# Sixteen dense tokens of the expert value stage are gathered, in packed form, instead of multiplied

## The chip, the cores and the metric

The kernel runs on one core of a Trainium2 chip and computes the whole step in one launch. The metric is the device time of that launch in microseconds (us). Before the change it was 4382.22 us, the median of three runs (4379.09 to 4385.64).

## The reference, cut to what matters

One layer of a hybrid decoder trunk is run for 576 tokens of width 2048 (512 of the prompt, 64 of eight samples). After the mixers (gated linear attention, mLSTM, S5) comes PEER, a layer of 16384 experts that are one neuron each. Every token has 8 heads, every head picks 16 experts, so a token has 128 picks:

```python
u_sel = jnp.take(u_tab, eidx, axis=0)
act = jax.nn.gelu(jnp.einsum('bhkd,bd->bhk', u_sel, xb))
v_sel = jnp.take(v_tab, eidx, axis=0)
return jnp.einsum('bhk,bhkd->bd', gate * act, v_sel)
```

`gate` is a softmax over the 16 scores of a head. Then `x = x + gate2 * out`, and a final RMSNorm over the 2048 channels.

## The kernel before, in words

All of the kernel's large products are made in three parts: each fp32 factor is split into a rounded high part and a low rest, and TensorE multiplies high by high, high by low and low by high, in the fp32r type. ScalarE writes the high parts, VectorE the low ones.

The kernel treats the 576 tokens in two ways. Tokens 0 to 319 (`TD` = 320) are **dense**; tokens 320 to 575 (256 of them, `TR`) are **rows**.

- First pass over the u table, `rows_product` (L2348 to L2362): for the 256 row tokens the activations of all 16384 experts are computed and saved to `row_activation_scratch`. Beside it VectorE picks the experts of all five token tiles in the order `ROUTED` = (3, 4, 0, 1, 2). Tiles 3 and 4 are the row tokens; their picks are written as indices (`row_ids`, `act_ids`). Tiles 0 to 2 cover the dense tokens.
- Second pass over the u table, `block_product`: 128 blocks of 128 experts, 48 matmuls each with 320 columns of dense tokens; ScalarE saves gelu of each block to `activation_scratch`. During its first 60 blocks (`GBLK * GL`) a matrix of gates, expert by token, is built for the dense tokens from one-hot matrices: VectorE makes them (`one_hots`, L1839 to L1845), TensorE multiplies them (L2429), ScalarE copies them out. PE may start block n only when VectorE has made its low part (`low`, L1719).
- Value stage (L2437 to L2462): the value table is read in 256 units (`UNITS`) of 128 experts by 1024 channels. A unit is 8 x 3 matmuls (L2457, L2458, L2459) with 320 columns, whose moving operands are the coefficients (gate times activation) of the dense tokens. Eight units make a round; after each, VectorE adds eight PSUM banks to `acc` (`add_half`, L1890). Per unit, SP loads the values (ring of six), ScalarE makes `ev_hi` (ring of four, L1204), VectorE makes `ev_lo` (L1869). Every second round also makes eight sets of coefficients (L1875, L1211, L1879).

The row tokens are **gathered**: for pick number s of 128, one token per partition, GpSimd (POOL) fetches one activation per partition (`act_column`, L793) and one value row of 2048 channels per partition (`value_rows`, L800). VectorE multiplies and adds them into `acc_rows` (`add_rows`, L1835, the first of a tile at L1832). That is 256 gathers (`NSP`) for two tiles of 128 tokens. POOL issues in the order of its program: 16 activation columns, then for each s the activation column s + 16 and the value rows s. All instructions of VectorE are in the order of the program too, and `add_rows` calls stand at fixed places in it: the first 56 (`NSP_GATES`) one behind each of the last 56 `low` calls of the 60 gate blocks, so behind that of b = 4 at first; up to number 148 (`NSP_EARLY`) in the remaining blocks of the second pass, the other 108 in the value stage, at most one per unit and only in units 2 to 6 of a round.

At the end TensorE transposes the gathered sums (`turn_rows`, twelve channel groups first, the last four between the sums of squares), VectorE scales both kinds of sum with `gate2` and adds them to x (L1919, L1931, L1935, L1936), TensorE sums the squares (L2480), VectorE scales the output (L1941).

Of the kernel before, what the change touches and what calls it, by code (L numbers as in the profile page):

```python
# [7 lines left out]
ALU = mybir.AluOpType  # L8
ACT = mybir.ActivationFunctionType
AX = mybir.AxisListType  # L10
F32 = mybir.dt.float32
# [22 lines left out]
TR = T - TD  # L34
RND = 8
UNITS = 2 * NK
RAWS, HIS, COS, ROWS = 6, 4, 11, 4
NSP, NSP_GATES, NSP_EARLY = 256, 56, 148
# [38 lines left out]
def build(nc, a, o):  # L77

    ctx = ExitStack()
    with ctx:  # L80
# [177 lines left out]
        gates = [attw[:, 128 * k:128 * k + 128] for k in range(2)]  # L258
        row_ids = [attw[:, 256 + 128 * k:384 + 128 * k].bitcast(U32) for k in range(2)]
        acts = [attw[:, 512:640], gla_mask[:, :].bitcast(F32)]  # L260
        act_ids = [cap[:, :].bitcast(U32), siluc[:, 0:128].bitcast(U32)]
        tcol = siluc[:, 128:130]
# [29 lines left out]
        acc_rows = [h_rest[:, :, TD + P * k:TD + P * k + P] for k in range(2)]  # L292
# [5 lines left out]
        smp = at(24064 + 2 * T, 4 * TS).rearrange("p (c b t) -> p c b t", c=4, t=SLEN)  # L298
        assert C0 + 12 * T <= C0 + ROWS * D and 8 * TD >= 4 * T
# [33 lines left out]
        act_table = rd.rearrange("k p (t o) -> (k p t) o", o=1)  # L333
        v_table = a["peer_v"].rearrange("i p d -> (i p) d")
# [61 lines left out]
        cols_made, idx_made, act_in = sem("cols_made"), sem("idx_made"), [sem(f"act{k}_in") for k in range(2)]  # L396
# [35 lines left out]
        VB = (6, 7, 4, 5, 0, 1, 2, 3)  # L432

# [73 lines left out]
        def _(sp):  # L507
# [118 lines left out]
            def load_factors(q):  # L626
                if q >= 2:
                    sp.wait_ge(co_lo_made, 4 * (q - 1))
                sp.dma_start(ag_acts[q % 2].rearrange("p (i t) -> p i t", t=TD), ad[:, 4 * q:4 * q + 4]
                             ).then_inc(ag_in[q % 2], 16)  # L630
                sp.dma_start(ag_gates[q % 2], gd[:, :, 4 * q:4 * q + 4, :]).then_inc(ag_in[q % 2], 16)
# [29 lines left out]
        def _(pool):  # L661
# [126 lines left out]
            pool.sem_inc(cols_made, 1)  # L788


            def act_column(c):
                k, s = c // P, c % P
                pool.indirect_dma_start(out=acts[k][:, s:s + 1], out_offset=None, in_=act_table,  # L793
# [3 lines left out]
            def value_rows(s):  # L797
                if row_clear(s):
                    pool.wait_ge(rows_used, row_clear(s))
                pool.indirect_dma_start(out=v_rows[row_place(s)], out_offset=None, in_=v_table,  # L800
                                        in_offset=bass.IndirectOffsetOnAxis(ap=row_ids[s // P][:, s % P:s % P + 1], axis=0)
# [17 lines left out]
        def _(act):  # L819
# [386 lines left out]
            def coefficient_high(n):  # L1206
# [4 lines left out]
                act.activation(co_hi[n % COS][:, :], ag_acts[n // 4 % 2][:, TD * (n % 4):TD * (n % 4) + TD], ACT.Copy  # L1211
                               ).then_inc(co_hi_made, 1)

            value_high(0)
# [23 lines left out]
        def _(dve):  # L1238
# [520 lines left out]
            for turn, n in enumerate(ROUTED):  # L1759
# [39 lines left out]
                if n < 3:  # L1799
                    ins.then_inc(sel_made, 1)  # L1800
                    next_low()
                    dve.wait_ge(sel_made, n + 1)
                    continue
                step(ins)
                next_low()
                dve.wait_ge(cols_made, 1)
# [13 lines left out]
            def add_rows(s):  # L1820

                if s == 0:
                    dve.wait_ge(blk_made, NB_ROWS)
                if s % ACOL == 0:
                    g, part = s // ACOL, slice(s % P, s % P + ACOL)
                    dve.wait_ge(act_in[g % 2], 16 * ACOL * (g // 2 + 1))
                    step(tt(acts[s // P][:, part], acts[s // P][:, part], gates[s // P][:, part], ALU.mult))
                k, col = s // P, acts[s // P][:, s % P:s % P + 1]
                row = v_rows[row_place(s)].rearrange("p (c t) -> p c t", t=P)
                dve.wait_ge(rows_in[row_sem(s)], row_fills(s))  # L1830
                if s in (0, P):
# [40 lines left out]
            def coefficients(q):  # L1872
                dve.wait_ge(ag_in[q % 2], 32 * (q // 2 + 1))
                x4 = ag_acts[q % 2].rearrange("p (i n t) -> p n i t", i=4, t=TBLK)
                tt(x4, x4, ag_gates[q % 2], ALU.mult).then_inc(co_made, 1)  # L1875

            def coefficient_low(n):
                dve.wait_ge(co_hi_made, n + 1)
                tt(co_lo[n % COS][:, :], ag_acts[n // 4 % 2][:, TD * (n % 4):TD * (n % 4) + TD],  # L1879
                   co_hi[n % COS][:, :].bitcast(F32), ALU.subtract).then_inc(co_lo_made, 1)  # L1880
# [677 lines left out]
```

## Time and profile before

| what | value |
|---|---|
| median of three runs | 4382.22 us |
| the profiled execution's own time | 4366.72 us |
| its span | 4365.0 us |
| PE busy | 4230.0 us (97%) |
| VectorE busy | 2829.1 us (65%) |
| ScalarE busy | 1289.3 us (30%) |
| POOL busy | 982.6 us (23%) |
| mean DMA rate | 228 GB/s |

The profile is of one execution. Its engines are PE (matmul), PEld (weight load, overlapping PE), DVE (VectorE), ACT (ScalarE), POOL (GpSimd), SP (the DMA queue of loads). "L12" is line 12 of the kernel. A matmul's duration overlaps the next one's, so the pace of matmuls is read from start to start. "DMA share" is the mean busy share of 16 DMA engines.

### The profile page before, as it was taken

Reading aid. Unit: us, or ns where it says so; the run is one execution under the profiler, and the core shown is the slowest. Engines: PE = TensorE matmul, PEld = TensorE weight load, DVE = VectorE, ACT = ScalarE, POOL = GpSimd, SP = SyncE. Lnnn points to the kernel's source line nnn. Section 1 sums busy time; section 2 is a strip of 40 time slices with the busy share of each in tenths; the row PEclk is TensorE's granted clock in tenths of the full one; section 3 lists DMA queues with packets and bytes.
Section 4 is the critical chain, followed back from the end, with each engine's and each line's share of the span. In section 5 each row is a group of like instructions: output and inputs, shape, how many; then the busy total and the mean of one; then the engine's idle time right before and its main releaser. Section 6 shows DMA issues by size and latency. Waiting matters only on the chain.

```text
span 4365.0 us, 63107 instructions
## 1 busy us (share of the span) xinstructions
PE 4230.0 (97%) x26448; PEld 3767.1 (86%) x26448; DVE 2829.1 (65%) x3861; ACT 1289.3 (30%) x1402; POOL 982.6 (23%) x627
## 2 busy tenths in 40 slices
PE   6999999999999899999999999999999999999997
PEld 3777777776689798777777999999999999999996
DVE  2488311322443424888888688877777688888885
ACT  2000101211221312443344444443333333333332
POOL 1000000001100100000000322228777355545430
PEclk8999999998889899999999999999999999999999
DMA  9211112127942223666666788889999999999984
GB/s 390 49 58 59 64 65 68 39 77 273 342 177 101 77 76 118 209 209 203 207 207 207 245 313 317 313 313 400 383 386 383 333 330 329 334 335 326 334 313 149
DMA packets 295940, 994.31 MB, mean 228 GB/s; under 512 B 42696, under 2 KB 112008, under 8 KB 233528
## 3 DMA queue, kind: packets, MB, share of 16 engines
q1 hardware_dynamic: 208728, 652.83, 42.9%
q0 software_dynamic: 48320, 279.88, 16.6%
q10 hardware_dynamic: 38688, 58.73, 3.6%
q8 instruction: 146, 2.39, 0.2%
q14 instruction: 58, 0.48, 0.0%
HBM read 917.71 MB, written 73.64 MB: 227 GB/s over the span
## 4 chain that ended last, share of the span: by engine, by line
PE 85%; DMA 7%; DVE 6%; ACT 2%; issue 0%; POOL 0%; SPq 0%; DVEq 0%; ACTq 0%
PE PS L2209 13%; PE PS L2334 8%; PE PS L2335 8%; PE PS L2336 8%; PE PS L2457 7%; PE PS L2459 7%; PE PS L2458 7%; PE PS L2212 5%; DMA arena<-in_peer_ut 5%; PE PS L2359 3%; DVE blk_lo L1719 3%; PE PS L2361 3%; PE PS L2360 3%; PE PS L1972 2%; PE PS L2429 2%; PE PS L2315 2%
## 5 line engine op out<-in xcount | busy, mean ns | idle before, releaser
L1719 DVE TENSOR_TENSOR blk_lo<-arena,blk_hi 128x2048 fp32r<-128x2048 f32 x272 | 623.3, 2292 | 252.6 <-ACT blk_hi L1093 249.8
L2334 PE MATMUL PS<-h_hi,blk_hi 128*128 128x320 f32 (+1 forms) x2496 | 773.7, 310 | 2.1 <-DVE blk_lo L1719 1.2
L2335 PE MATMUL PS<-h_lo,blk_hi 128*128 128x320 f32 (+1 forms) x2496 | 765.9, 307 | 0.0
L2336 PE MATMUL PS<-h_hi,blk_lo 128*128 128x320 f32 (+1 forms) x2496 | 765.8, 307 | 0.0
L800 POOL DMA_INDIRECT arena<-in_peer_v,attw x256 | 486.6, 1901 | 806.7 <-DVE arena L1835 729.5
L1093 ACT ACTIVATE blk_hi<-arena 128x2048 fp32r<-128x2048 f32 x272 | 520.7, 1914 | 401.1 <-DMA arena<-in_peer_ut 400.1
L2457 PE MATMUL PS<-co_hi,ev_hi 128*128 128x320 f32 x2048 | 634.3, 310 | 4.7 <-DVE ev_lo L1869 2.5
L2458 PE MATMUL PS<-co_lo,ev_hi 128*128 128x320 f32 x2048 | 633.8, 309 | 0.0
L2459 PE MATMUL PS<-co_hi,ev_lo 128*128 128x320 f32 x2048 | 633.7, 309 | 0.0
L2209 PE MATMUL PS<-arena 128*128 128x288 f32 x2176 | 552.4, 415 | 2.1 <-DVE arena L1278 2.1
L2209 PEld LDWEIGHTS PS<-arena 128*128 128x128 f32 x2176 | 417.6, 194 | 121.0 <-issue 2.6
L2334 PEld LDWEIGHTS PS<-h_hi,blk_hi 128*128 128x128 f32 x2496 | 470.1, 188 | 3.9 <-issue 1.9
L2335 PEld LDWEIGHTS PS<-h_lo,blk_hi 128*128 128x128 f32 x2496 | 470.0, 188 | 0.0
L2336 PEld LDWEIGHTS PS<-h_hi,blk_lo 128*128 128x128 f32 x2496 | 469.5, 188 | 0.0
L1204 ACT ACTIVATE ev_hi<-arena 128x1024 fp32r<-128x1024 f32 x256 | 271.8, 1062 | 568.5 <-DMA arena<-in_peer_v 318.9
L2359 PE MATMUL PS<-blk_hi,h_hi 128*128 128x512 f32 x1024 | 408.4, 399 | 21.2 <-DVE blk_lo L1719 21.1
L793 POOL DMA_INDIRECT attw<-row_activation_scratch,cap x128 | 183.3, 1432 | 999.3 <-DMA row_activation_scratch<-arena 960.5
L2360 PE MATMUL PS<-blk_hi,h_lo 128*128 128x512 f32 x1024 | 400.1, 391 | 0.0
L2361 PE MATMUL PS<-blk_lo,h_hi 128*128 128x512 f32 x1024 | 400.0, 391 | 0.0
L2457 PEld LDWEIGHTS PS<-co_hi,ev_hi 128*128 128x128 f32 x2048 | 385.0, 188 | 5.5 <-DVE ev_lo L1869 3.1
L2458 PEld LDWEIGHTS PS<-co_lo,ev_hi 128*128 128x128 f32 x2048 | 385.0, 188 | 0.0
L2459 PEld LDWEIGHTS PS<-co_hi,ev_lo 128*128 128x128 f32 x2048 | 384.9, 188 | 0.0
(455 smaller groups left out, 5992.7 us busy)
## 6 DMA issues: line engine op xcount, KB each, us to landing
arena<-in_peer_ut SPq DMA_DIRECT2D x256, 1024.0 KB, 6.0
arena<-in_peer_v SPq DMA_DIRECT2D x256, 512.0 KB, 6.9
arena<-in_w_ada SPq DMA_DIRECT2D x38, 2048.0 KB, 11.3
arena<-in_w_f SPq DMA_DIRECT2D x17, 2048.0 KB, 7.9
activation_scratch<-arena ACTq DMA_DIRECT2D x128, 160.0 KB
gate_scratch<-arena ACTq DMA_DIRECT2D x10, 2048.0 KB, 14.4
arena<-activation_scratch SPq DMA_DIRECT2D x32, 640.0 KB, 7.7
arena<-gate_scratch SPq DMA_DIRECT2D x32, 640.0 KB, 11.0
```

Of the source, the lines that this page charges most:

```text
L1093: act.activation(blk_hi[k][:, :], blk_raw[k], ACT.Copy).then_inc(blk_hi_made, 1)
L1719: tt(blk_lo[k][:, :], blk_raw[k], blk_hi[k][:, :].bitcast(F32), ALU.subtract).then_inc(blk_lo_made, 1)
L2209: ins = mm(bank(job % 2, 0, HALF), w[:, c, P * (j // 2):P * (j // 2) + P], hT[:, c, HALF * (j % 2):HALF * (j % 2) + HALF], start=c == 0, s ...
L2334: mm(out, hi[:, c], h_part[0][:, c, cols], start=c == 0, stop=False)
L2335: mm(out, hi[:, c], h_part[1][:, c, cols], start=False, stop=False)
L2336: ins = mm(out, lo[:, c], h_part[0][:, c, cols], start=False, stop=c == KC - 1)
L2359: mm(out, h_part[0][:, 4 * q + c, tok], hi[:, c], start=first, stop=False)
L2360: mm(out, h_part[1][:, 4 * q + c, tok], hi[:, c], start=False, stop=False)
L2361: ins = mm(out, h_part[0][:, 4 * q + c, tok], lo[:, c], start=False, stop=last)
L2457: mm(out, ev_hi[k % HIS][:, w], co_hi[n % COS][:, :], start=i == 0, stop=False)
L2458: mm(out, ev_hi[k % HIS][:, w], co_lo[n % COS][:, :], start=False, stop=False)
L2459: ins = mm(out, ev_lo[k % RAWS][:, w], co_hi[n % COS][:, :], start=False, stop=i == RND - 1)
```

## The change

Tokens 304 to 319 (`NX` = 16) leave the dense value product, which now has 304 columns (`TV`), and are gathered as well. Sixteen tokens with 128 picks each are 2048 rows, packed as 16 gathers of 128 partitions: partition 16 g + t holds a pick of token t, and eight groups of partitions take eight picks of each token at a time. So there are 272 gathers. Numbers 208 to 223 are the new ones.

- After tile 2 is routed, VectorE computes row index, activation index and gate for it (five small instructions), and POOL packs them with eight small DMAs. These stand in POOL's program after its first 16 activation columns and before the first value rows.
- The activations of the sixteen tokens are fetched from `activation_scratch`, which still holds all 320 columns; the u pass is not changed, nor are the loads of coefficients (ten groups of 32 tokens).
- `NSP_GATES` goes from 56 to 58 and `NSP_EARLY` from 148 to 152, so the first `add_rows` stands behind the `low` of b = 2, and 120 of them are in the value stage.
- At the end a matmul with a fixed 128 x 16 matrix (`part_sum`) adds the eight groups of partitions for each of 16 channel groups, and VectorE adds the result to x. The turned rows use eight slots of PSUM in place of twelve, so groups 8 to 11 wait for the first quarter of VectorE's final sums, and groups 12 to 15 for the second.

```diff
-NSP, NSP_GATES, NSP_EARLY = 256, 56, 148
+NSP, NSP_GATES, NSP_EARLY = 256 + NX, 58, 152
+X_FIRST = 208
...
-            pool.wait_ge(sel_made, 3)
+            pool.wait_ge(idx_made, 3)
+            lo = TV - TILE_AT[2]
+            for g in range(XPARTS):
+                pool.dma_start(packed[NX * g:NX * g + NX].rearrange("p (r k) -> p r k", k=NX),
+                               unpacked[lo:lo + NX, :, NX * g:NX * g + NX]).then_inc(pack_in, 16)
             for s in range(NSP):
+                if s + ACOL == X_FIRST:
+                    pool.wait_ge(pack_in, 16 * XPARTS)
+                    for k in range(3):
+                        pool.wait_ge(a_saved[k], saves(NB_ALL)[k])
                 if s + ACOL < NSP:
                     act_column(s + ACOL)
...
-                    out, w = bank(VB[c], 0, TD), slice(P * c, P * c + P)
-                    mm(out, ev_hi[k % HIS][:, w], co_hi[n % COS][:, :], start=i == 0, stop=False)
+                    out, w = bank(VB[c], 0, TV), slice(P * c, P * c + P)
+                    mm(out, ev_hi[k % HIS][:, w], co_hi[n % COS][:, 0:TV], start=i == 0, stop=False)
...
             def turn_rows(c):
-                slot = c % 12
-                if c >= 12:
-                    pe.wait_ge(fin_made, 1)
+                slot = c % 8
+                if c in (8, 12):
+                    pe.wait_ge(fin_made, c // 4 - 1)
+                mm(bank(4 + c // 4 % 2, NX * (c % 4), NX), acc_rows[2][:, c], part_sum, start=True, stop=True)
...
+                step(tt(few, bank(4 + q % 2, 0, 4 * NX).rearrange("p (c t) -> p c t", t=NX),
+                        mod[:, 80 + 4 * q:84 + 4 * q, 0:1].broadcast_to([P, 4, NX]), ALU.mult))
+                tt(xg[q][:, :, TV:TD], xg[q][:, :, TV:TD], few, ALU.add)
```

## Rows read from the trace of the kernel before

**Rows 1.** Page, part 4: the chain that ended last, by engine.
```profile
PE 85%; DMA 7%; DVE 6%; ACT 2%; issue 0%; POOL 0%; SPq 0%; DVEq 0%; ACTq 0%
```

**Rows 2.** Windows: gate blocks, rest of second pass, value stage; columns in the first line.
```profile
core 0: us, PE busy (x) PEld busy (x) DVE busy (x) ACT busy (x) POOL busy (x), PEclk, DMA share, GB/s
3412.30:4317.90 905.60, 903.00 (x6144) 902.41 (x6144) 746.81 (x785) 317.54 (x382) 410.09 (x191) 1.00 0.88 319
2435.10:2934.00 498.90, 498.90 (x3559) 498.90 (x3558) 422.25 (x359) 227.84 (x203) 150.29 (x129) 1.00 0.84 306
2934.00:3411.00 477.00, 474.89 (x3228) 473.03 (x3226) 363.43 (x166) 154.69 (x134) 354.94 (x192) 1.00 0.99 385
```

**Rows 3.** Timeline of PE, query blocks: start us, us, instruction; 256, then 320 columns.
```profile
1554.64 0.28 PE L2335 MATMUL PS<-h_lo,blk_hi 128*128 128x256 f32 x1
...
1560.28 0.31 PE L2334 MATMUL PS<-h_hi,blk_hi 128*128 128x320 f32 x1
...
1567.32 1.27 PE L2370 MATMUL PS<-arena 128*128 x10
```

**Rows 4.** Timeline of POOL: first gathers, and two plain DMAs earlier.
```profile
924.85 0.53 POOL L752 DMA_DIRECT2D out_m_s<-arena  x1
...
2457.06 1.90 POOL L793 DMA_INDIRECT attw<-row_activation_scratch,cap  x1 [0.30 <-issue]
...
2460.51 0.97 POOL L793 DMA_INDIRECT attw<-row_activation_scratch,cap  x1 [0.30 <-issue]
...
2469.40 0.94 POOL L800 DMA_INDIRECT arena<-in_peer_v,attw  x1 [0.30 <-issue]
```

**Rows 5.** Timeline of DVE, start of the gate blocks.
```profile
2455.86 2.29 DVE L1719 TENSOR_TENSOR blk_lo<-arena,blk_hi 128x2048 fp32r<-128x2048 f32 x1
...
2470.24 2.29 DVE L1719 TENSOR_TENSOR blk_lo<-arena,blk_hi 128x2048 fp32r<-128x2048 f32 x1 [1.97 <-ACT blk_hi L1093]
...
2476.35 1.29 DVE L1832 TENSOR_SCALAR arena<-arena,attw 128x2048 f32<-128x2048 f32 x1 [3.73 <-DMA arena<-in_peer_v,attw]
2477.55 0.69 DVE L1843 TENSOR_TENSOR arena<-iota,arena 128x512 f32<-128x512 f32 x1
```

**Rows 6.** Timeline of ACT there: the gelu behind the end of block b = 3.
```profile
2467.97 0.44 ACT L1104 ACTIVATE arena<-PS 128x320 f32<-128x320 f32 x1 [0.70 <-PE PS L2336]
```

**Rows 7.** PE after a long idle time: timeline, and the window behind it.
```profile
1467.24 0.55 PE L2394 MATMUL PS<-h_hi,blk_hi 128*128 128x256 f32 x1 [15.54 <-DVE h_lo L1713]
...
1467.20:1472.30 5.10, 5.06 (x21) 5.09 (x22) 4.75 (x5) 5.10 (x7) 0.00 (x0) 0.50 0.00 0
```

**Rows 8.** Timeline of ACT and PE at unit 21 of the value stage.
```profile
3488.23 1.06 ACT L1204 ACTIVATE ev_hi<-arena 128x1024 fp32r<-128x1024 f32 x1 [9.45 <-DMA arena<-in_peer_v]
...
3490.60 0.42 PE L2457 MATMUL PS<-co_hi,ev_hi 128*128 128x320 f32 x1
```

**Rows 9.** Windows: one round without and one with coefficients to make.
```profile
3469.00:3497.00 28.00, 27.98 (x191) 27.72 (x190) 20.36 (x19) 8.49 (x8) 11.91 (x10) 1.00 0.99 368
3497.00:3525.00 28.00, 28.00 (x193) 28.00 (x192) 26.55 (x31) 11.20 (x16) 15.68 (x7) 1.00 0.88 306
```

**Rows 10.** DMA view of 3440 to 4290 us: packets, MB, share; issues and us to landing.
```profile
q0 software_dynamic: 17587, 108.06, 32.5%
...
arena<-in_peer_v,attw POOLq DMA_INDIRECT x103, 10.0
```

**Rows 11.** Groups by line of 3440 to 4290 us: busy, mean ns, idle before.
```profile
L1835 DVE SCALAR_TENSOR_TENSOR arena<-arena,gla_mask 128x2048 f32<-128x2048 f32 x107 | 251.1, 2347 | 0.2
```

**Rows 12.** Timeline, the end (DVE, PE) and a matmul with 8 columns.
```profile
1035.62 1.95 PE L2282 MATMUL PS<-arena 128*128 128x8 f32 x16
...
4313.79 3.79 DVE L1919 SCALAR_TENSOR_TENSOR arena<-arena,modT 128x320 f32<-128x320 f32 x8 [7.39 <-DMA arena<-x_scratch]
...
4322.07 0.42 DVE L1931 TENSOR_TENSOR arena<-PS,modT 128x256 f32<-128x256 f32 x1 [1.32 <-PE PS L2471]
...
4325.03 1.29 PE L2480 MATMUL PS<-arena,ones 128*128 128x512 f32 x4 [1.31 <-ACT arena L1233]
```

More of the change, by code:

```diff
@@ L34 @@
 TR = T - TD
+NX = 16
+TV = TD - NX
+XPARTS = P // NX
+VGROUPS = -(-TV // TBLK)
 RND = 8
@@ L257, in build @@
         e_f, a_f = p_rep[:, 0:P], p_rep[:, P:2 * P]
[L258 to L262, printed above, removed]
+        packed = scaleg[:, 0:3 * NX]
+        gates = [attw[:, 128 * k:128 * k + 128] for k in range(2)] + [packed[:, 2 * NX:3 * NX]]
+        row_ids = [attw[:, 256 + 128 * k:384 + 128 * k].bitcast(U32) for k in range(2)] + [packed[:, 0:NX].bitcast(U32)]
+        acts = [attw[:, 512:640], gla_mask[:, :].bitcast(F32), scaleg[:, 3 * NX:4 * NX]]
+        act_ids = [cap[:, :].bitcast(U32), siluc[:, 0:128].bitcast(U32), packed[:, NX:2 * NX].bitcast(U32)]
+        tcol = siluc[:, 128:131]
+        unpacked = at(R1, 3 * P).rearrange("p (r k) -> p r k", k=P)
+        part_sum = silu32[:, 0:NX]
         p_sv = sel_all[:, 0:256].rearrange("p (h s k) -> p h s k", s=2, k=TOPK)
@@ L291, in build @@
         h_rest = at(KC * T, KC * T).rearrange("p (c t) -> p c t", t=T)
-        acc_rows = [h_rest[:, :, TD + P * k:TD + P * k + P] for k in range(2)]
+        acc_rows = [h_rest[:, :, TD + P * k:TD + P * k + P] for k in range(2)] + [h_rest[:, :, 0:P]]
         v_rows = [at(C0 + D * k, D) for k in range(ROWS + 1)]
@@ L395, in build @@
         ev_made, vp_made, acc_made = sem("ev_made"), sem("vp_made"), sem("acc_made")
-        cols_made, idx_made, act_in = sem("cols_made"), sem("idx_made"), [sem(f"act{k}_in") for k in range(2)]
+        pack_in, idx_made, act_in = sem("pack_in"), sem("idx_made"), [sem(f"act{k}_in") for k in range(2)]
         rows_in = [sem(f"rows{k}_in") for k in range(ROWS)]
@@ L787, in _ @@
                                allow_small_or_imprecise_dtypes=True))
-            pool.sem_inc(cols_made, 1)
+            step(pool.iota(tcol[:, 2:3], [[0, 1]], base=TILE_AT[2], channel_multiplier=1,
+                           allow_small_or_imprecise_dtypes=True))
+            step(pool.tensor_copy(part_sum, ident[:, 0:NX]))
+            for g in range(1, XPARTS):
+                step(pool.tensor_tensor(part_sum, part_sum, ident[:, NX * g:NX * g + NX], ALU.add))
+            pool.sem_inc(consts_made, 1)
             def act_column(c):
-                k, s = c // P, c % P
-                pool.indirect_dma_start(out=acts[k][:, s:s + 1], out_offset=None, in_=act_table,
+                k, s = row_of(c)
+                pool.indirect_dma_start(out=acts[k][:, s:s + 1], out_offset=None, in_=act_table if k < 2 else dense_table,
                                         in_offset=bass.IndirectOffsetOnAxis(ap=act_ids[k][:, s:s + 1], axis=0)
@@ L797, in value_rows @@
             def value_rows(s):
+                k, col = row_of(s)
                 if row_clear(s):
```

55 lines of the change are left out of this document (36 added, 19 removed).

## The prediction

> **What bounds the kernel now.** I read the chain of waits first: 85% of it is PE [rows 1]. Then the windows by stage. In the gate blocks PE is busy all 498.9 us, in the rest of the second pass 474.9 of 477.0, in the value stage 903.0 of 905.6 [rows 2]. So what matters there is how long a matmul takes, and whether something makes PE wait. The other columns show what stands close behind: in the rest of the second pass the DMA engines are busy 0.99 of the time at 385 GB/s, in the value stage 0.88, and VectorE there 746.8 of 905.6 us.
>
> **Fewer columns.** Matmuls overlap, so their pace is the distance of starts. In the query blocks the same instructions run with both widths: 47 steps of 256 columns take 1560.28 - 1554.64 = 5.64 us, 120.0 ns each; 48 steps of 320 columns take 1567.32 - 1560.28 = 7.04 us, 146.7 ns each [rows 3]. That is 0.417 ns per column, so 304 columns take 146.7 - 16 x 0.417 = 140.0 ns. The value stage has 6144 of them (905.6 / 6144 = 147.4, the same pace [rows 2]). Gain: 6144 x 6.67 ns = **-41.0 us**. A unit falls from 3.52 to 3.36 us, a round from 28.2 to 26.9. The widths on both sides were measured; only if the pace had a step between 256 and 320 columns could the gain be 0 or 164 us, and neither end is near.
>
> **The first gather meets an earlier place in VectorE's order.** This is the term that I take to be most important after the columns. Before, the first `add_rows` stands behind the low part of b = 4, which starts at 2470.24, and VectorE still waits 3.73 us for the first rows (2476.35) [rows 5]. Now it stands behind that of b = 2, which starts at 2455.86 and ends at 2458.1. But POOL does not start earlier: its first column waits for the saved activations of the first pass. Column 10 starts at 2457.06, column 12 at 2460.51, and each costs 0.94 and 0.30 between them where nothing disturbs it; at that pace from column 11 (2459.3) on, column 16 ends at 2466.4. Then come the eight packing DMAs, 0.53 us each by a plain small one: 4.3 us; one more column 1.25; the first value rows 1.25, issued at 2473.2 [rows 4]. Before, the rows were issued at 2470.34 and VectorE went on 6.0 us later [rows 4, 5]. So they land at about 2479.2, with little other traffic perhaps 1.5 us earlier.
>
> VectorE executes in order, and behind the waiting `add_rows` stand the one-hots (three instructions of 0.7) and the low part for block b = 4 of the gate blocks. PE has finished block 3 at about 2467.6, by the gelu of 2467.97 [rows 6], and needs that low part then. It gets it at 2479.2 + 1.2 (first multiply) + 2.1 (one-hots) + 2.3 (low) = 2484.8: PE idles 17.2 us; with the faster landing 15.7. I take 16.5, bounds 12 and 21 (packing DMAs of 0.3 to 1.0 us). After 15.5 us without work PE ran at a granted clock of 0.50 (1.2 GHz) for 5.1 us [rows 7]; half of that is lost, 2.5 us. Nothing gives this back, as PE is busy all the time afterwards [rows 2]. **+19 us.** The next blocks: VectorE owes per block one low part 2.2, one `add_rows` 2.3 and 4/3 one-hots 2.8 us, 7.3 in all, against some 8 us of PE, so no second stall. The five instructions at the end of routing (some 1.5 us) lie where VectorE waits for ScalarE; nothing.
>
> **Two more gathers in the rest of the second pass** (94 for 92). A gather with its column costs 32.5% of 850 us over 103, 2.7 us of all DMA engines [rows 10]; two are 5.4 us in 477 that are 0.99 full [rows 2]. The bounds are 0 (the rows only queue longer; POOL is four ahead) and 6. I take **+2**, since PE there loses 2 us of 477 at this load.
>
> **Twelve more gathers in the value stage** (120 for 108). On VectorE each is 2.26 us (2347 ns, of which 0.09 overlap [rows 11]): +27, and the narrower sums and coefficients give back 6. So 768 of 864.6 us, 89% for 82%. A round with coefficients had 26.55 us of work in 28 [rows 9]; with 0.37 more gathers and 16 narrower instructions (0.3) it has 27.1 against 26.9. The round without them has 20.4 and takes the rest. VectorE is up to three units ahead, so alone it costs about nothing (0 to 3).
>
> The DMA engines are the closer matter. Their share was 0.88 x 905.6 = 797 us, plus 12 x 2.7 = 829 of 864.6: 0.96. But rounds differ: where coefficients are loaded the engines are busy 0.99 of a round at 368 GB/s, in the other 0.88 [rows 9]. In the full ones loads arrive late already: at unit 21 the cast starts at 3488.23 after waiting 9.45 us for its load, and the unit's first matmul, at 3490.60, lasts 0.42 where the others of its kind last 0.31 [rows 3, 8]: it had to wait a little, there is no reserve at all. A round shorter by 1.3 us with 1.0 us (0.37 x 2.7) more to move makes loads 2.3 us later. Reading the casts against PE's units in all sixteen such rounds, four had under 2 us of reserve and ten over 3; so four lose about 2 us each and a few some tenths. I take **+7**, bounds 0 and 16.
>
> One rule of the Trainium skill speaks against the change: its page "DMA: Bandwidth & Descriptors", section "Specifications", gives about 358 GB/s as the limit that HBM sets per core. By it the full rounds (368 x 28 us = 10.3 MB, plus 0.4) would need 29.9 us instead of 26.9, and the stage would lose some 48 us rather than 7. The trace does not agree: it moved 385 GB/s over 477 us [rows 2].
>
> **The end.** The loads of x are issued six units before the end and land when VectorE then still has 3.8 us of work before its last half round [rows 12]; six units are now 1.0 us shorter, the sums 0.3 shorter: +0.7. Each channel group now has one more fp32 matmul with 16 columns. Sixteen instructions of eight such matmuls with 8 columns took 1.95 us, so 0.23 each [rows 12]. Four of them delay VectorE's first quarter (4322.07) by 0.9, two more small instructions cost 0.5, and that quarter takes 2.2; the four groups that now wait for its end (4325.7) take 0.45 each, and the sums of squares begin at 4327.6, not at 4325.03 [rows 12]: +2.6, and 4 x 0.23 between them. In all **+4.2** with x, bounds 2 and 7.
>
> **Sum.** -41.0 + 19 + 2 + 7 + 4.2 = -8.8 us against the profiled time of 4366.7. That execution was 15.5 us under the median of the runs; the difference carries over unchanged, so 4382.2 - 8.8 = **4373.4**, say 4373. From the bounds (the terms' ends rarely come together) the case's own range is 4358 to 4388.
>
> **Rivals.**
> 1. *The transfers bound the value stage* (slower). Full rounds can't lend to the others, because the ring of loads is only six units deep. Each of sixteen stays at its 28 us times 0.99 plus 1.0 = 28.7 in place of 26.9: 29 us lost, where I put 7. 4373 + 22 = 4395. For: rows 8 and 9. Against: 385 GB/s was possible [rows 2], so the 10.7 MB need only 27.8. The change is slower by more than 0.2% once the stage's losses pass 25 us.
> 2. *The first gather is hidden*: POOL or the activations come earlier, or PE has more low parts in stock than I read. Then 19 goes: 4354. For: the wait of 3.73 us before hurt nobody. Against: PE needs the low part right behind the waiting instruction.
> 3. *The value stage keeps its pace*, with the stall at the first gather as forecast: 4366. For: the second pass runs at 0.99 with PE hardly waiting [rows 2].
> 4. *Columns don't set the pace in this stage*, so 304 cost what 320 do (the change doesn't do what it says): 4414. Against: rows 3.
> 5. *Full rounds stay at the rate they had*, rival 1 in a sharper form: 10.7 MB at the 368 GB/s of [rows 9] are 29.1 us, 2.2 lost in each of sixteen, 35 in place of 7: 4401. The page "DMA: Bandwidth & Descriptors" of the Trainium skill (Specifications) would set that rate at 358.
>
> **How the numbers follow.** Forecast 0.55, rival 1 0.10, rival 5 0.02, rival 2 0.15, rival 3 0.15, rival 4 0.03. A measurement can tell some 0.2%, 9 us, from no change. Faster (under 4373.4): half of the forecast's case 0.28, rival 2 0.15, rival 3 0.11 = 0.54. Slower (over 4391): 0.02 of the forecast, and 0.13 of the 0.15 of rivals 1, 4 and 5 (a mild rival 1 stays below) = 0.15. The same: 0.31. The range for 8 in 10 reaches from just below rival 2, 4351, to 4391; what lies above is rivals 1, 4 and 5, and half of rival 2's own spread lies below.
>
> **What would show it.** In the changed profile: starts 140 ns apart in the value stage, a unit of 3.36 us; one idle time of PE of 12 to 21 us about 30 us into the gate blocks, released by a low part, with POOL's eight DMAs between its columns and the first rows, and a clock of 0.50 behind it; VectorE waiting some 20 us for gathered rows before the first multiply; in the value stage idle times of 1 to 3 us before L2457, five or six units into every second round; an end longer by 4 us. The prediction is wrong if PE doesn't idle at the first gather, or if the value stage takes less than 866 or more than 885 us.

## The result, and the profile after

The changed kernel takes **4406.05 us** (median of 4 runs, 4404.45 to 4413.27); the kernel before took 4380.66 us beside it on the same chip (4373.50 to 4385.64). The ratio is 1.0054, with a 95% interval of 1.0040 to 1.0067: the change is **slower by 0.54%**, 25 us. Forecast were 4373 us and a range up to 4391.

The chain of waits after, to be held against [rows 1]: PE's share fell from 85% to 76%, and the DMAs' rose from 7% to 12%.

```profile
PE 76%; DMA 12%; DVE 8%; ACT 2%; issue 1%; POOL 1%; SPq 0%; DVEq 0%; ACTq 0%; POOLq 0%
```

The windows of the three stages after, cut by the same instructions: gate blocks, rest of the second pass, value stage.

```profile
core 0: us, PE busy (x) PEld busy (x) DVE busy (x) ACT busy (x) POOL busy (x), PEclk, DMA share, GB/s
2443.50:2954.70 511.20, 498.69 (x3520) 497.25 (x3520) 424.76 (x360) 224.48 (x202) 155.66 (x141) 0.99 0.82 299
2954.70:3439.90 485.20, 480.37 (x3268) 478.81 (x3266) 371.00 (x170) 158.38 (x138) 363.33 (x196) 1.00 0.99 388
3439.90:4347.00 907.10, 869.63 (x6144) 860.76 (x6144) 761.58 (x795) 315.08 (x382) 443.87 (x215) 0.98 0.91 331
```

The border between the first two stages is here the last matmul that writes gates, 5.7 us earlier than in [rows 2]; cut alike, the kernel before had 493.2 and 484.0 us. So the spans compare like this (us):

| stretch | before | after | difference | forecast |
|---|---|---|---|---|
| start to gate blocks | 2435.1 | 2443.5 | +8.4 | 0 |
| gate blocks | 493.2 | 511.2 | +18.0 | +19 |
| rest of second pass | 484.0 | 485.2 | +1.2 | +2 |
| value stage | 905.8 | 907.1 | +1.3 | -34 |
| end | 46.9 | 55.7 | +8.8 | +4.2 |

The 8.4 us at the start are a difference of executions. In the twelve experiments below that point lies anywhere between 2434.2 and 2443.7, and three that are the kernel before up to the value stage (e2, e7, e12) have 2442.0, 2439.1 and 2434.2. Without it the traces differ by 29 us, the medians by 25.

**The first gather** cost what was forecast. The timeline of POOL after: the first column, the sixteenth, the eight packing DMAs, one column more, the first value rows.

```profile
2451.90 1.10 POOL L815 DMA_INDIRECT attw<-row_activation_scratch,cap  x1 [954.52 <-DMA row_activation_scratch<-arena]
...
2473.67 0.94 POOL L815 DMA_INDIRECT attw<-row_activation_scratch,cap  x1 [0.30 <-issue]
2474.62 4.17 POOL L835 DMA_DIRECT2D scaleg<-arena  x8
2479.09 1.01 POOL L815 DMA_INDIRECT attw<-row_activation_scratch,cap  x1 [0.30 <-issue]
2480.41 0.99 POOL L823 DMA_INDIRECT arena<-in_peer_v,attw  x1 [0.31 <-issue]
```

VectorE there: it waits for the columns, then for the rows, and only then makes the low part of the next block.

```profile
2476.78 0.17 DVE L1868 TENSOR_TENSOR attw<-attw 128x16 f32<-128x16 f32 x1 [9.23 <-DMA attw<-row_activation_scratch,cap]
2486.04 1.29 DVE L1873 TENSOR_SCALAR arena<-arena,attw 128x2048 f32<-128x2048 f32 x1 [9.09 <-DMA arena<-in_peer_v,attw]
...
2489.30 2.28 DVE L1751 TENSOR_TENSOR blk_lo<-arena,blk_hi 128x2048 fp32r<-128x2048 f32 x1
```

PE is released by that low part, here first in this kernel, then in the experiment `e6_spread`, which has the same code up to there. The changed kernel's 9.74 us lie below the 12 to 21 that the prediction gave for one idle time: in this execution PE had already lost some microseconds to five short gaps (2.8 us) and a low clock in the block ahead of the wait. In the six experiments with the same code up to there (e3, e4, e5, e6, e8, e9) it is one idle time of 15.8 to 16.0 us. All seven have gate blocks of 510.9 to 512.1 us.

```profile
2491.71 0.63 PE L2378 MATMUL PS<-h_hi,blk_hi 128*128 128x320 f32 x1 [9.74 <-DVE blk_lo L1751]
```

```profile
2490.49 0.63 PE L2378 MATMUL PS<-h_hi,blk_hi 128*128 128x320 f32 x1 [15.78 <-DVE blk_lo L1751]
```

**The value stage** is where the expected gain is missing. PE's starts there, each with the idle time ahead of it: five of fourteen places that lie some two rounds apart.

```profile
3681.91 0.41 PE L2501 MATMUL PS<-co_hi,ev_hi 128*128 128x304 f32 x1 [2.27 <-DVE ev_lo L1910]
3740.95 0.62 PE L2501 MATMUL PS<-co_hi,ev_hi 128*128 128x304 f32 x1 [5.56 <-DVE ev_lo L1910]
3797.44 0.41 PE L2501 MATMUL PS<-co_hi,ev_hi 128*128 128x304 f32 x1 [0.99 <-DVE ev_lo L1910]
3857.07 0.62 PE L2501 MATMUL PS<-co_hi,ev_hi 128*128 128x304 f32 x1 [5.59 <-DVE ev_lo L1910]
3918.48 0.62 PE L2501 MATMUL PS<-co_hi,ev_hi 128*128 128x304 f32 x1 [5.95 <-DVE ev_lo L1910]
```

The view of PE's waits over the stage (engine, instruction, releaser: us in total, times, longest) sums them:

```profile
PE PS L2501 <- DVE ev_lo L1910: 37.0, 26, 5.9
PE PS L2501 <- issue: 3.5, 1, 3.5
```

The 3.5 us of the second line lie just ahead of the stage's first matmul, so the idle time inside it is 37.0 us. Nearly all of it comes once in some 56 us, in the round in which coefficients are loaded, as rival 1 has it. VectorE is named, but it only passes the wait on. At the idle time that ends at 3740.95 it waited 6.96 us for ScalarE, and ScalarE 9.40 us for the values themselves, which SyncE had asked for from 3718.90 on, right behind two loads of factors. ScalarE, VectorE and SyncE there:

```profile
3738.59 1.06 ACT L1235 ACTIVATE ev_hi<-arena 128x1024 fp32r<-128x1024 f32 x1 [9.40 <-DMA arena<-in_peer_v]
```

```profile
3739.67 1.23 DVE L1910 TENSOR_TENSOR ev_lo<-arena,ev_hi 128x1024 fp32r<-128x1024 f32 x1 [6.96 <-ACT ev_hi L1235]
```

```profile
3716.90 0.33 SPq L646 DMA_DIRECT2D arena<-activation_scratch  x1
3717.27 0.89 SPq L648 DMA_DIRECT2D arena<-gate_scratch  x1
3718.90 16.86 SPq L639 DMA_DIRECT2D arena<-in_peer_v  x6
```

The DMA engines are wholly busy for a whole round before such an idle time. The windows of 28 us that end at the last two shown above (a share over 1 comes of counting each transfer in the window in which it starts):

```profile
3830.00:3858.00 28.00, 22.41 (x160) 22.16 (x160) 16.74 (x21) 7.10 (x7) 12.97 (x9) 0.95 1.02 393
3891.50:3919.50 28.00, 22.05 (x157) 21.81 (x156) 17.20 (x19) 6.36 (x6) 14.15 (x11) 0.95 1.02 393
```

The idle time is not the whole loss. The windows at and behind the one that ends at 3740.95: the DMA engines move 394 GB/s while PE waits, then PE runs 5.2 us at a granted clock of 0.51, which is its level of 1.2 GHz, and returns to 1.00.

```profile
3735.50:3741.10 5.60, 0.14 (x1) 0.15 (x1) 1.39 (x3) 1.06 (x1) 0.00 (x0) 0.83 1.00 394
3740.90:3746.10 5.20, 5.14 (x20) 5.15 (x21) 5.04 (x4) 3.18 (x3) 2.15 (x2) 0.51 0.70 280
3746.10:3752.00 5.90, 5.90 (x45) 5.90 (x44) 5.90 (x8) 2.93 (x4) 4.88 (x3) 1.00 0.92 290
```

Summed over windows of 5 us, (1 - clock) x time makes 18 us for this stage; it made 1.7 before. Some of that falls into the idle times themselves (the first window above has 0.83) and costs nothing more. The starts of all 6144 matmuls, held against a pace of 137.8 ns, give the whole: 41 us are lost at the waits, 14 us at the low clock and 5 us in steps too short to show as waits, 60 us together.

**The end.** VectorE's last work with x, then PE's first turn and the first of the sums of squares, against [rows 12]:

```profile
4344.10 3.66 DVE L1960 SCALAR_TENSOR_TENSOR arena<-arena,modT 128x304 f32<-128x304 f32 x8 [7.94 <-DMA arena<-x_scratch]
```

```profile
4350.96 0.58 PE L2513 MATMUL PS<-silu,arena 128*128 128x16 f32 x2 [3.98 <-DVE arena L1931]
...
4360.17 2.23 PE L2525 MATMUL PS<-arena,ones 128*128 128x512 f32 x4
```

The window behind that idle time of 3.98 us has a clock of 0.51; the one at the same place before had 1.00.

```profile
4351.00:4364.00 13.00, 13.00 (x58) 11.32 (x59) 8.96 (x28) 1.94 (x3) 0.00 (x0) 0.51 0.01 1
```

```profile
4317.90:4325.00 7.10, 2.98 (x26) 2.61 (x24) 5.68 (x16) 0.71 (x2) 0.00 (x0) 1.00 0.00 1
```

### The profile page after: what moved, and what is told of

Its sections match the earlier page's. It is cut to its first block, busy times and chain, and to the rows that moved or that the text cites. A ratio compares the mean times of both kernels' runs of the same rounds, so it can differ in the third digit from the quotient of the medians.

```text
span 4402.7 us, 63270 instructions
## 1 busy us (share of the span) xinstructions
PE 4216.6 (96%) x26480; PEld 3741.5 (85%) x26480; DVE 2857.1 (65%) x3891; ACT 1286.7 (29%) x1402; POOL 1036.4 (24%) x676
## 4 chain that ended last, share of the span: by engine, by line
PE 76%; DMA 12%; DVE 8%; ACT 2%; issue 1%; POOL 1%; SPq 0%; DVEq 0%; ACTq 0%; POOLq 0%
PE PS L2253 13%; PE PS L2378 7%; PE PS L2379 7%; PE PS L2380 7%; DMA arena<-in_peer_v 5%; PE PS L2256 5%; DMA arena<-in_peer_ut 4%; PE PS L2501 4%; PE PS L2503 4%; PE PS L2502 4%; PE PS L2403 3%; PE PS L2405 3%; PE PS L2404 3%; DVE blk_lo L1751 3%; PE PS L2016 2%; PE PS L2359 2%
## 5 line engine op out<-in xcount | busy, mean ns | idle before, releaser
L2501 PE MATMUL PS<-co_hi,ev_hi 128*128 128x304 f32 x2048 | 623.8, 305 | 41.0 <-DVE ev_lo L1910 37.0
L823 POOL DMA_INDIRECT arena<-in_peer_v,attw x256 | 461.6, 1803 | 729.9 <-DVE arena L1876 652.1
L2503 PE MATMUL PS<-co_hi,ev_lo 128*128 128x304 f32 x2048 | 620.8, 303 | 0.0
L2502 PE MATMUL PS<-co_lo,ev_hi 128*128 128x304 f32 x2048 | 618.4, 302 | 0.0
L2378 PEld LDWEIGHTS PS<-h_hi,blk_hi 128*128 128x128 f32 x2496 | 471.1, 189 | 15.2 <-issue 13.4
```

Source lines behind the costliest of these rows:

```text
L2378: mm(out, hi[:, c], h_part[0][:, c, cols], start=c == 0, stop=False)
L2501: mm(out, ev_hi[k % HIS][:, w], co_hi[n % COS][:, 0:TV], start=i == 0, stop=False)
L2502: mm(out, ev_hi[k % HIS][:, w], co_lo[n % COS][:, 0:TV], start=False, stop=False)
L2503: ins = mm(out, ev_lo[k % RAWS][:, w], co_hi[n % COS][:, 0:TV], start=False, stop=i == RND - 1)
```

## The experiments

Each kernel was timed against the kernel before, on the same chip. Ratios are to that kernel, with their 95% intervals; on these chips it had medians of 4372.6 to 4373.8 us. The changed kernel's ratio is 1.0054.

### The first gather: e1_late_first

VectorE's first `add_rows` goes back behind the low part of b = 4; two later blocks take two each.

```
-                if b >= GBLK * GL - NSP_GATES:
+                for _ in range((b >= 4) + (b in (30, 45))):
                     add_rows(placed)
                     placed += 1
```

> The changed kernel with one edit: the first gathered row is added behind the low part of block b = 4, as before the change, and blocks 30 and 45 add two rows each, so that still 58 are added in the gate blocks. If the idle time of PE of some 15 us in the gate blocks comes from the earlier place of the first add, it goes, and with it the half clock behind it: about 17 us less than the changed kernel, 4389. If POOL's eight packing DMAs alone made it, a stall of some 5 us stays (the rows come 5 us later than before the change, when VectorE waited 3.7 us for them without harm) and the gain is 10 us or so. The value stage stays at about 907 us by every theory.

Measured: 4390.9 us, ratio 1.0043 [1.0026, 1.0060]. The interval overlaps the changed kernel's, so the gain, 5 us by the ratios, is read from the traces: the gate blocks take 501.1 us instead of 511.2, and the long idle time is gone. The place in VectorE's order made 10 of the 18 us. The expectation had 17 for the place alone, and 10 for the case that POOL's packing DMAs have a part. The other 8 stay: PE idles 2.57, 2.49 and 0.62 us there, and runs 3.4 us at the lower clock behind the second. Only the first, at 2495.39, belongs to the first gather: VectorE again waits 6.8 us for its rows. The other two come when VectorE is still behind after the blocks with two adds each, so they are the edit's own. No run leaves the packing out. PE's waits in the value stage are 35.5 us, for 37.0 before the edit: the two losses are independent.

### Each half of the change alone: e2_cols_only and e3_gathers_only

e2 is the kernel before with 304 columns in the value products and no gather added. It leaves out the values of 16 dense tokens.

```
+TV = TD - 16
-                    out, w = bank(VB[c], 0, TD), slice(P * c, P * c + P)
-                    mm(out, ev_hi[k % HIS][:, w], co_hi[n % COS][:, :], start=i == 0, stop=False)
+                    out, w = bank(VB[c], 0, TV), slice(P * c, P * c + P)
+                    mm(out, ev_hi[k % HIS][:, w], co_hi[n % COS][:, 0:TV], start=i == 0, stop=False)
...
(co_hi, co_lo, the half sums and add_dense with TV alike)
```

> The kernel before with 304 columns in the value products and nothing else: the values of tokens 304 to 319 are left out, no gather is added. Theory A (late transfers: shorter rounds and more bytes both bring the rounds that load coefficients beyond the transfers): most of the 41 us arrives, but some stalls of 1 to 2 us appear, value stage 866 to 880 us, total 4342 to 4355. Theory B (VectorE can't do its work in a round of 26.9 us): with 108 adds it has 741 of 865 us, so no stall, 865. Theory C (the narrower matmul doesn't pay): stage stays at 905.

e3 is the changed kernel with its gathers, and products, `co_hi` and `co_lo` with all 320 columns.

```
-                    mm(out, ev_hi[k % HIS][:, w], co_hi[n % COS][:, 0:TV], start=i == 0, stop=False)
+                    mm(out, ev_hi[k % HIS][:, w], co_hi[n % COS][:, 0:TD], start=i == 0, stop=False)
...
```

> The changed kernel with the value products at 320 columns again, whose last 16 columns nobody uses; all 272 gathers, the packing and the end stay. Theory A: rounds of 28.2 us leave the transfers 1.3 us more, so the stalls fall from 34 us to some 10 and the clock stays up; value stage 915 us for 906.8 of the changed kernel, total about 4414. Theory B: VectorE has room, stage 907. If the gathers alone make the stalls, stage 940.

Measured: e2 4351.9 us, 0.9959 [0.9944, 0.9973]; e3 4411.7 us, 1.0084 [1.0068, 1.0101]. The windows of their value stages, and PE's waits in e2 and then in e3:

```profile
3417.80:4298.10 880.30, 859.13 (x6144) 854.63 (x6144) 736.40 (x782) 315.12 (x382) 402.94 (x191) 0.99 0.90 328
```

```profile
3436.60:4357.60 921.00, 907.20 (x6144) 905.63 (x6144) 772.88 (x798) 316.87 (x382) 432.70 (x215) 0.99 0.90 327
```

```profile
PE PS L2458 <- DVE ev_lo L1870: 21.1, 14, 4.7
```

```profile
PE PS L2501 <- DVE ev_lo L1910: 13.8, 5, 5.1
```

The narrower products alone gain 25.5 us of the stage (905.8 to 880.3) and already bring 21 us of idle time, with not a byte added. The gathers alone cost 15.2 (to 921.0) where PE is slower, and 26.8 (880.3 to 907.1) where it is faster. So the price of a gather isn't a constant: it depends on how fast PE asks for the next values.

### Bytes or VectorE: e4_half_gathers, e5_half_adds, e9_narrow_rows

VectorE works more too, so the late low parts could be its own. e5 halves VectorE's work for each gathered row in the value stage (the sums over the second half of the columns are left out) and leaves the transfers as they are.

```
...
+                    cs = slice(0, KC if s < NSP_EARLY else KC // 2)
+                    ins = stt(acc_rows[k][:, cs], row[:, cs], col, acc_rows[k][:, cs], ALU.mult, ALU.add)
```

> The changed kernel, but in the value stage VectorE adds only the first 1024 of the 2048 channels of each gathered row; all transfers are made in full. Theory A (the loads of values come late in rounds that also load coefficients): VectorE has 120 x 1.1 = 130 us less to do, the casts still wait for their loads, value stage stays within 10 us of 907. Theory B (VectorE is late): the stalls go, stage 865, total about 4365.

e4 halves the transfers another way: in the value stage it gathers rows for 64 of the 128 partitions (the picks of the others are left out), with VectorE's work unchanged.

```
+                h = P if s < NSP_EARLY else P // 2
+                pool.indirect_dma_start(out=v_rows[row_place(s)][0:h], out_offset=None, in_=v_table,
+                                        in_offset=bass.IndirectOffsetOnAxis(ap=row_ids[k][0:h, col:col + 1], axis=0)
...
```

> The changed kernel, but in the value stage each gather fetches the rows of 64 of the 128 tokens only; the other half of the buffer keeps older rows, so those sums are left out. VectorE and PE do all their work. Theory A (transfers): 120 x 1.35 = 160 us less for the DMA engines, no stall, value stage 862 to 868 and total about 4360. Theory B (VectorE): stage stays near 907, total 4406.

e9 gathers half of each row for all 128 partitions in the value stage (the second half of the columns is not fetched), with VectorE's work unchanged.

```
+        v_halves = a["peer_v"].rearrange("i p (h d) -> (i p h) d", h=2)
...
+                late = s >= NSP_EARLY
+                pool.indirect_dma_start(out=v_rows[row_place(s)][:, 0:D // 2 if late else D], out_offset=None,
+                                        in_=v_halves if late else v_table,
...
```

> The changed kernel, but in the value stage every gather fetches rows of 1024 channels, half the bytes, for all 128 partitions (so the sums of those rows are left out), and all else is done in full. It takes the place of e4_half_gathers, whose transfers to 64 partitions kept the engines 0.94 busy at 256 GB/s and so did not unload them. Theory A: 120 x 0.52 = 63 MB less, value stage 862 to 870, total about 4365. Theory B (VectorE): the stage stays near 907.

Measured: e5 4388.3 us, 1.0033 [1.0018, 1.0048]; e4 4426.7 us, 1.0119 [1.0103, 1.0136]; e9 4350.7 us, 0.9946 [0.9929, 0.9962]. The windows of the three value stages, in the order e5, e4, e9:

```profile
3438.60:4330.50 891.90, 861.84 (x6144) 856.77 (x6144) 641.39 (x795) 312.97 (x382) 343.30 (x215) 0.99 0.92 337
```

```profile
3431.90:4370.00 938.10, 875.89 (x6144) 863.18 (x6144) 760.21 (x795) 313.31 (x382) 441.00 (x215) 0.98 0.94 256
```

```profile
3435.40:4290.60 855.20, 850.65 (x6146) 848.89 (x6144) 762.82 (x795) 316.60 (x383) 467.67 (x215) 1.00 0.84 281
```

120 us less for VectorE (761.6 to 641.4) gain 15 us, more than the 10 that theory A allowed. Against e8, whose value stage has the changed kernel's code and took 902.3 us, it is 10, and by the ratios 9 with intervals that touch. Half of the gathered bytes, with VectorE as busy as in the changed kernel (762.8), gain 52 us, and what remains of PE's waits is this. (Two rounds of e9, 27 us each from 3700 on, have DMA shares of 0.91 and 0.78, and PE is busy in all of both.)

```profile
PE PS L2504 <- DVE ev_lo L1913: 4.1, 2, 3.9
```

The DMA view shows why, for 3440 to 4290 us (packets, MB, share of the 16 engines), first of the changed kernel, then of e9, then of e4: in e9 the queue of the gathers falls from 36.1% to 20.4%. The loads of values take 5.1 us from issue to landing in e9, 6.9 in the kernel before, 7.8 in e2, 8.9 in e5.

```profile
q1 hardware_dynamic: 79256, 166.65, 56.4%
q0 software_dynamic: 19872, 121.70, 36.1%
```

```profile
q1 hardware_dynamic: 81609, 177.82, 63.2%
q0 software_dynamic: 19872, 60.88, 20.4%
```

```profile
q1 hardware_dynamic: 76599, 160.93, 65.2%
q0 software_dynamic: 12282, 59.81, 30.9%
```

e4 looks like a contradiction: it moves the fewest bytes of all (256 GB/s) and is the slowest. The share column resolves it: its engines are busy 0.94 of the time. Gathers to half of the partitions halve the bytes of their queue (121.70 to 59.81 MB) and its share only from 36.1% to 30.9%, while the share of the loads' queue grows from 56.4% to 65.2% with fewer bytes. I had taken bytes and engine time for one thing when I designed it. The runs don't show why; e4 ranks with the rest by time of the engines alone.

### The burst of loads: e6_spread and e7_before_spread

The factors of a round are loaded close together, twice in a pair of rounds, ahead of the values. e6 moves every second of these loads four units later; e7 is the same edit in the kernel before.

```
-                    if co_step(4 * q - 5) + 4 == k:
+                    if co_step(4 * q - 5) + (8 if q % 2 and q > 4 else 4) == k:
```

> The changed kernel with one number edited: the second of the two loads of coefficients in each pair of rounds is issued four units later, so that they are 27 us apart in place of 13. The bytes are the same. Theory A in the form that the burst makes the stalls (two coefficient loads of 1.3 MB each, 13 us apart, in front of the value loads on the same queue): the stalls of PE shrink from 37 us to under 10 and the clock stays up; value stage 870 to 885, total 4370 to 4385. Theory A2 (the mean rate is at its limit, 96% of the engines): nothing is gained by moving, stage 900 to 910. Theory B (VectorE): 907.

> The kernel before with the same one edit, the second coefficient load four units later. PE hardly waited in its value stage (4.6 us in 905.8), so every theory expects the same time within 0.2%, 4370 to 4380 beside the kernel before; a slower one would mean that the later place makes VectorE wait for the coefficients.

Measured: e6 4399.8 us, 1.0058 [1.0042, 1.0075]; e7 4377.6 us, 1.0013 [1.0002, 1.0024]. In e6 the waits are more and shorter (31 for 26, the longest 3.8 us for 5.9), their sum hardly changes (34.3 us for 37.0), and the stage takes 901.8 us for 907.1, where e8 with the changed kernel's code took 902.3. So the edit gains nothing that can be told from a difference of executions: the burst decides where the loss lies, and not how much it is.

### The gathers moved away: e10_moved

Fourteen gathers go from the value stage to the gate blocks, whose DMA share is only 0.82; it builds on e1's order.

```
-NSP, NSP_GATES, NSP_EARLY = 256 + NX, 58, 152
+NSP, NSP_GATES, NSP_EARLY = 256 + NX, 72, 166
-                if b >= GBLK * GL - NSP_GATES:
+                for _ in range((b >= 4) + (b in range(8, 56, 3))):
```

> The changed kernel with the first add behind block b = 4 as in e1, and 14 more gathers moved from the value stage (120 to 106) to the gate blocks (58 to 72: two adds behind every third block from 8 on), where the DMA engines are 0.84 busy. The rest of the second pass keeps 94. If the mean load of transfers sets the value stage, as e9 has it, then going from 120 to 106 full gathers (37 us of engine time) takes it from 907 to some 880 (e2 had 108 and 880), and the gate blocks stay at 501 us or below; total about 4364. If the gate blocks can't bear it (VectorE has 7.9 us of work per 8.2), they lengthen by more than 5 us.

Measured: 4400.4 us, 1.0072 [1.0055, 1.0088]. The value stage falls to 876.5 us, 29 less than e1's; the gate blocks rise to 542.9 from e1's 501.1. Their waits, of PE and of VectorE:

```profile
PE PS L2378 <- DVE blk_lo L1751: 33.3, 18, 5.1
```

```profile
DVE arena L1876 <- DMA arena<-in_peer_v,attw: 51.6, 19, 6.6
```

VectorE waits 51.6 us for rows (10.3 in e1), with low parts queued behind, and POOL's busy time rises from 163 to 237 us. The gathers help the stage that they leave, as expected, and cost more in the one they enter: it is the expectation's other case, with 42 us where more than 5 would have shown it. Why the rows come late there, with the DMA engines busy 0.86 of the time, was not tried.

### The end: e8_tail, e12_before_tail, e11_moved_tail

e8 puts the last half round's sum ahead of the wait for x and of the first eight `add_dense`, so that the turns needn't wait for these; e12 does so in the kernel before, e11 on top of e10.

```
+            add_half(2 * NK // RND - 1)
             dve.wait_ge(x_in, 96)
...
             for c in range(RND):
                 add_dense(c)
-            add_half(2 * NK // RND - 1)
```

> The changed kernel with one edit at the end: VectorE adds the last eight PSUM banks to its sums before it waits for x and adds the first eight channel groups to it, not after. Theory: PE idles 4.0 us there in the changed kernel (2.8 before the change) and its turns then run at a granted clock of 0.5, which is half of the 8.8 us by which the end grew (55.7 us for 46.9). With the edit PE idles about 0.6 us, the clock stays at 1.0, the turns of the first eight groups run beside the adds of x: end 48 to 50 us, total 6 to 7 us less than the changed kernel. Rival: the end grew only through the 16 added matmuls and the later start of the sums of squares, the clock being a sampling accident; then 3 us of idle go and no more, end 52 to 53.

> The kernel before the change with the edit of e8_tail alone. PE idles 2.8 us there and keeps its full clock, so only the order is gained: the turns begin 2.5 us earlier and VectorE's first quarter some 2 us earlier, total 2 us less (0.05%), hard to tell from none.

> e10_moved and e8_tail together, the version that the experiments point to: value stage about 880, end about 49, total about 4358, some 15 us under the kernel before.

Measured: e8 4392.0 us, 1.0045 [1.0028, 1.0063]; e12 4373.8 us, 1.0002 [0.9994, 1.0011]; e11 4398.0 us, 1.0057 [1.0044, 1.0070]. The ends take 52.2, 48.7 and 51.9 us, where they took 55.7 in the changed kernel and 46.9 in the one before. e11 was expected near 4358 us and missed it for the same reason as e10: its gate blocks take 548.5 us, its value stage the expected 878.8. PE in e8, and the windows from its first turn on:

```profile
4338.35 0.36 PE L2513 MATMUL PS<-silu,arena 128*128 128x16 f32 x2 [0.65 <-DVE arena L1931]
...
4344.31 0.60 PE L2513 MATMUL PS<-silu,arena 128*128 128x16 f32 x2 [2.58 <-DVE arena L1980]
```

```profile
4338.35:4343.90 5.55, 3.38 (x32) 3.14 (x32) 5.48 (x16) 0.00 (x0) 0.00 (x0) 1.00 0.00 0
4343.90:4351.00 7.10, 6.69 (x25) 5.33 (x26) 6.89 (x22) 1.94 (x3) 0.00 (x0) 0.52 0.01 2
```

The idle time before the first turn falls from 3.98 to 0.65 us, and these turns run at full clock. But then PE waits 2.58 us for VectorE's first quarter, because only eight slots are there for turned rows, and the clock falls all the same, for half as long. So the end takes the 52 us that the expectation's rival gave, though the turns did run faster, and the total isn't told apart from the changed kernel's (the intervals overlap). In the kernel before, the turns begin 2.4 us earlier too (4318.47 for 4320.90), but the first sum of squares does not (4324.89 for 4325.03): PE waits 3.61 us for ScalarE there, the clock falls, and the edit gains nothing.

None of these kernels that computes the whole reference is faster than the kernel before; e2 and e9 are, and both leave work out.

## Why the prediction was wrong, step by step

**The step that failed is "Twelve more gathers in the value stage", taken at +7 us with bounds 0 and 16.** By the prediction's own frame (864.6 us for the stage with narrower columns and nothing else) the gathers cost 42 us. The mechanism stands in the prediction, as rival 1: full rounds that can't lend to the others. It was given 29 us there and 0.10 of the chance.

What had been worked out right is the time of the DMA engines: 829 us expected, 0.91 x 907.1 = 825 measured. What was wrong is how much a stage loses at such a share. I had read the reserves in the sixteen full rounds and charged each for a delay of 2.3 us, so that only the four with under 2 us of reserve should lose. The casts tell otherwise. Take as reserve the time from the end of a unit's cast to its first matmul, less the 1.23 us of the low part between, and its lowest value in each of the sixteen pairs of rounds. Before, seven were under 2 us and nine over 3. In the changed kernel fourteen are at 0.1 us, in e2 ten, in e9 none. So in eight pairs a reserve of 3 to 5 us was used up as well, which a delay of 2.3 us would have left standing. The experiments give a relation for the whole stage. Divide the engines' busy time by the stage at PE's pure pace (6144 starts at 137.8 ns make 846.6 us; with 320 columns at 146.7 ns, 901.3 us), and put the loss, stage less pure pace, beside it. The shares have two digits, so the quotient is good to 0.01:

| kernel | DMA busy / pure pace | loss, us |
|---|---|---|
| e9_narrow_rows | 0.85 | 8.6 |
| before | 0.88 | 4.5 |
| e3_gathers_only | 0.92 | 19.7 |
| e2_cols_only | 0.94 | 33.7 |
| e10_moved | 0.94 | 29.9 |
| e5_half_adds | 0.97 | 45.3 |
| changed kernel | 0.97 | 60.5 |
| e4_half_gathers | 1.04 | 91.5 |

The other six lie among them: e7 0.90 and 5.6, e12 0.89 and 4.0, e11 0.93 and 32.2, e1 0.97 and 58.5, e6 0.97 and 55.2, e8 0.97 and 55.7. Up to 0.90 the stage loses 4 to 9 us; from there on each hundredth costs about 6 us. e4, which moves the fewest bytes, falls into line. VectorE's load seems to be a second, smaller cause: at 0.97 the kernel with 120 us less work on VectorE loses 10 to 15 less than the others. Both halves of the change push the same way: fewer columns shorten the denominator, more gathers raise the numerator. That the time of the DMA engines decides is shown by e9 and e5 (one taken away at a time), by e4 (bytes without the time) and by the order of the fourteen; the relation holds for this stage only. Why the rest of the second pass stands a share of 0.99 with PE busy 480 of 485 us was not tried and stays open. It had misled me: I had used it against rivals 1 and 5.

Part of the 60 us has no term in the prediction at all: 14 us of lower clock. The prediction priced half a clock after the long idle time at the first gather, from [rows 7], and not after the short ones that it expected in the value stage.

**Fewer columns**: too small. 304 columns start 137.8 ns apart, not 140.0, as 147 steps in e9 show:

```profile
3700.00 0.30 PE L2504 MATMUL PS<-co_hi,ev_hi 128*128 128x304 f32 x1
...
3720.25 0.30 PE L2504 MATMUL PS<-co_hi,ev_hi 128*128 128x304 f32 x1
```

So the products became shorter by 901.3 - 846.6 = 54.7 us, not 41.0: the interpolation between 120.0 and 146.7 isn't straight. The gain was real and was then lost whole, 54.7 against a loss that grew from 4.5 to 60.5 (55.7 in e8).

**The first gather**: right, +18.0 for +19. The idle time was worked out as 16.5 us; six of seven traces have 15.8 to 16.0, the changed kernel's own a shorter one beside other losses. The columns were later than read (the first at 2451.90, the sixteenth ending at 2474.6, where 2466.4 was forecast), but so was the whole stage by 8.4 us. The packing took 4.17 us for the forecast 4.3, and VectorE waited 9.23 + 9.09 = 18.3 us for the forecast "some 20". Of the 18 us the later place in e1 saves 10.

**Two more gathers in the rest of the second pass**: right, +1.2 for +2.

**The end**: +8.8 for +4.2, outside the bounds of 2 to 7. The waits came where they were described, and an added matmul takes less than the 0.23 us forecast (0.14 at full clock in e8); unpriced was the clock. PE idled 3.98 us before the first turn, 2.84 before the change, and ran at 0.51 for 13 us. Over the whole end (1 - clock) x time is some 16 us, 9 before, both with the last stretch, where PE has no work.

**The rivals.** 1 and 5 (transfers bound the stage): the place and cause, with 29 and 35 us for the 42 measured in the same frame; rival 5's rate of 368 GB/s is no limit, as the engines moved 393 GB/s in the two full rounds shown, and 388 over the whole rest of the second pass. The page "DMA: Bandwidth & Descriptors" of the Trainium skill (Specifications) gives some 358 GB/s as the limit per core; the rows of this kernel, which runs on one core, lie above it. By that rate alone, an estimate with the page's figure, the whole stage's 331 GB/s x 907.1 us = 300 MB would need 839 us, less than it took. So it was not the mean rate that bound the stage, but full rounds in which the engines have no time left (a share of 1.02 in the two shown). That the ring of loads, six units deep, is what keeps them from lending to the others is argued; no run has another depth. 2 (first gather hidden): refuted by the timeline. 3 (the stage keeps its pace): refuted by the 907 us; e9, at 855, is what it would have looked like. 4 (columns set no pace): refuted by e2.

**What would show it**: the idle times in the value stage reach 5.95 us where 1 to 3 were named, and the stage took 907 us, above the 885 that the prediction named as its own refutation.

The sum of the measured terms: -54.7 + 56.0 (value stage's losses) + 18.0 + 1.2 + 8.8 = +29.3 us, against +25.4 between the medians.

## What to carry to other kernels

A stage whose DMA engines are 0.88 busy behind a PE that is never idle can be without room on either side: divide the DMA engines' busy time by the time that the stage will have. In this stage, whose load changes from round to round, each hundredth past 0.9 cost about 6 us; in the rest of the second pass 0.99 cost little, so such a number is to be measured for each stage. Reserves of 3 to 5 us did not help in rounds that needed all the time of the DMA engines. Making the bounding engine faster is itself such a load; test it alone (here by leaving the columns out) before paying for it with transfers. And price long idle times of PE twice, once for themselves and once for the clock that can follow: here one of 5.56 us was followed by 5.2 us at 0.51.

## What the runs showed of the hardware

- Idle times of PE of 5.56 us and more in the value stage were each followed by some 5 us at a granted clock of 0.5, and so was the 3.54 us ahead of the stage; the ones of 2.27 and 0.99 us shown above were not, and after one of 1.91 us, at 3570.81, a window of 5 us still had 0.71. So the length of one idle time alone doesn't tell it: at the end, 3.98 us was, and in e8 2.58 us was, after turns that had kept PE busy only 3.38 of 5.55 us.
- fp32r matmuls of 256, 304 and 320 columns started 120.0, 137.8 and 146.7 ns apart: 0.37 ns per column between the first two, 0.56 between the last two.
- The DMA engines moved 388 GB/s over 485 us of the second pass, reads and writes together, and 394 in a stretch of 5.6 us.
- Gathers of 8 KB rows to 64 partitions moved fewer bytes (256 GB/s for 331) and the engines were busier (0.94 for 0.91); gathers of 4 KB rows to 128 partitions brought the queue's share from 36.1% to 20.4%.
- Eight small DMAs between parts of the on-chip memory cost POOL 4.17 us to issue, 0.52 each.
